# Streaming encoder step on 8 cores: the sums of squares of an RMS norm are joined on GpSimd ahead of one averaging matmul, and the planner's tables change with it

## The reference

```python
def rms_norm(x, g):
    y = x * rsqrt(mean(x * x, axis=-1, keepdims=True) + EPS)
    return y * g

def trunk_layer(x, c, ...):
    sh_m, sc_m, gt_m, sh_f, sc_f, gt_f = split(dot(silu(c), w_ada) + b_ada, 6)
    h = rms_norm(x, g_mix) * (1 + sc_m) + sh_m
    z = dot(h, w_in)                      # p | u | v
    u, v = gelu(z_u), layer_norm(gelu(z_v))
    mix = dot(concat([pool_mixer(p), u * (w_s v + b_s)]), w_out)
    x = x + gt_m * mix
    h = rms_norm(x, g_ffn) * (1 + sc_f) + sh_f
    x = x + gt_f * dot(silu(dot(h, w_gate)) * dot(h, w_up), w_down)
# after four layers: y = rms_norm(x, g_final)
```

## Time and profile before

| what | value |
|---|---|
| median of 3 runs | 2673.65 us (2672.88 to 2675.32) |
| the profiled execution | 2672.88 us |
| its span on core 0, the slowest | 2671.3 us |
| spans of the even cores | 2671.3, 2670.2, 2668.7, 2667.3 us |
| spans of the odd cores | 2661.4, 2661.7, 2662.1, 2660.4 us |
| busy on core 0 | PE 97%, DVE 62%, ACT 39%, POOL 8% |

### The profile page before, as it was taken

The page is one execution under the profiler, slowest core; times in us unless marked ns, Lnnn a source line. Parts: engine busy times, 40 slices in busy tenths (PEclk is TensorE's granted clock), DMA queues, the critical chain, the costliest instruction groups (busy, mean ns, idle before and its releaser), DMA issues.

```text
span 2671.3 us, 51741 instructions; the slowest of 8 cores (2660.4 to 2671.3 us)
## 1 busy us (share of the span) xinstructions
PE 2600.9 (97%) x18083; PEld 1575.1 (59%) x18083; DVE 1658.1 (62%) x3481; ACT 1032.0 (39%) x1737; POOL 216.6 (8%) x382
## 2 busy tenths in 40 slices
PE   5899999999999999999999999999999999999997
PEld 4666655555577655555557655555556765545645
DVE  2898654445789854444679885444467986444457
ACT  3676211113678611111477741111167872111144
POOL 2111000000001100000001110000001110000022
PEclk9999999999999999999999999999999999999999
DMA  9943653451010364551201055456101023111112
GB/s 182 210 80 62 116 98 64 80 95 33 1 37 5 89 124 80 93 97 18 48 1 37 5 116 112 80 96 111 32 1 36 6 53 64 29 32 28 29 48 84
DMA packets 31398, 174.23 MB, mean 65 GB/s; under 512 B 3696, under 2 KB 5424, under 8 KB 16544
## 3 DMA queue, kind: packets, MB, share of 16 engines
q0 software_dynamic: 23744, 148.87, 30.1%
q1 hardware_dynamic: 6704, 20.37, 2.4%
q10 hardware_dynamic: 688, 1.61, 0.2%
HBM read 302.41 MB, written 9.67 MB: 117 GB/s over the span
## 4 chain that ended last, share of the span: by engine, by line
PE 91%; DMA 2%; issue 2%; DVE 2%; ACT 1%; POOL 1%; POOLq 0%; DVEq 0%; ACTq 0%
PE bank L655 91%; DMA rows<-b_s 2%; ACT heap L878 0%; DMA wps<-w_ps 0%; DVE heap L870 0%; DVE x_sb L903 0%; DVE heap L835 0%; DVE x_sb L914 0%; POOL heap L647 0%; ACT heap L830 0%; DVE heap L875 0%; POOL rv L1003 0%; DVE heap L1102 0%; POOL rv L1005 0%; DVE heap L909 0%
## 5 line engine op out<-in xcount | busy, mean ns | idle before, releaser
L655 PE MATMUL bank<-heap 128*128 128x512 bf16 (+5 forms) x15272 | 2502.3, 326 | 9.6 <-DVE heap L1102 2.6
L655 PEld LDWEIGHTS bank<-heap 128*128 128x128 bf16 (+1 forms) x15272 | 1456.6, 98 | 998.3 <-issue 23.6
L903 DVE SCALAR_TENSOR_TENSOR x_sb<-bank,modT,x_sb 128x256 f32<-128x256 f32 (+2 forms) x1216 | 705.2, 592 | 497.7 <-PE bank L655 495.0
L1206 ACT ACTIVATE heap<-bank 128x512 bf16<-128x512 f32 (+4 forms) x447 | 228.9, 516 | 1253.6 <-PE bank L655 1139.9
L1208 DVE TENSOR_TENSOR heap<-heap,bank 128x512 bf16<-128x512 bf16 (+4 forms) x447 | 262.2, 587 | 287.4 <-PE bank L655 266.6
L878 ACT ACTIVATE heap<-heap,modT,gsc 128x256 bf16<-128x256 f32 (+1 forms) x335 | 174.0, 579 | 61.7 <-DVE heap L870 45.1
L870 DVE TENSOR_TENSOR heap<-x_sb,heap 128x512 f32<-128x512 f32 (+1 forms) x272 | 168.5, 655 | 38.4 <-ACT heap L854 24.4
L835 DVE TENSOR_TENSOR heap<-heap 128x512 f32<-128x512 f32 (+3 forms) x300 | 156.9, 542 | 30.2 <-ACT heap L830 21.7
L830 ACT ACTIVATE heap<-x_sb 128x1024 f32<-128x1024 f32 (+3 forms) x119 | 120.7, 1025 | 98.9 <-DVE x_sb L903 60.6
L1003 POOL TENSOR_SCALAR rv<-mv 128x1 f32<-128x1 f32 (+1 forms) x68 | 24.5, 360 | 740.0 <-DVE mv L1002 692.2
L661 ACT ACTIVATE heap<-bank 128x512 bf16<-128x512 f32 (+3 forms) x126 | 70.5, 588 | 34.0 <-PE bank L655 28.6
(11 more groups left out here) (80 smaller groups left out, 897.9 us busy)
## 6 DMA issues: line engine op xcount, KB each, us to landing
heap<-w_ada POOLq DMA_DIRECT2D x47, 1024.0 KB, 9.3
heap<-w_gate POOLq DMA_DIRECT2D x15, 1024.0 KB, 8.8
heap<-w_up POOLq DMA_DIRECT2D x15, 1024.0 KB, 13.0
heap<-w_down POOLq DMA_DIRECT2D x15, 1024.0 KB, 17.3
heap<-w_in POOLq DMA_DIRECT2D x9, 1024.0 KB, 11.1
heap<-w_out POOLq DMA_DIRECT2D x8, 1024.0 KB, 10.4
heap<-crow SPq DMA_DIRECT2D x15, 512.0 KB, 6.0
y_out<-heap SPq DMA_DIRECT2D x14, 512.0 KB, 2.6
```

Of the source, the lines that this page charges most:

```text
L655: r = e.matmul(s[0], s[1], s[2], start=s[3], stop=s[4], **(s[5] if len(s) > 5 else {}))
L903: dve(lambda e: e.scalar_tensor_tensor(out=xv, in0=B(bk)[:, 0:np_], scalar=modT[:, m, base + n, 0:1], in1=xv, op0=ALU.mult, op1=ALU.add), ...
L1206: act(lambda e: e.activation(out=sv(), in_=B(bks[0])[:, 0:N], func=AF.Silu), 0.067 + N / 1200, [bks[0].res[0]], [sg.res[0]], "silu")
```

## The change

Two tables of numbers change, and no code. The one number that changes what is computed where is ADD, from 4 to 8 in both roles:

```diff
     0: dict(RES_MIX=44000, RES_FFN=20000, RATE_A=0.7, RATE_B=0.6, HOLD=2, BOOST=20.0, SCARCE=1, SWITCH=6.0,
-            SLACK=2.0, LEAD_S=16.0, LEAD_H=10.0, LEAD_F=4.0, ADD=4, BUS0=12.5, FILL=2.2, HM0=4,
+            SLACK=1.0, LEAD_S=16.0, LEAD_H=4.0, LEAD_F=2.0, ADD=8, BUS0=12.5, FILL=2.2, HM0=4,
```

More of the change, by code:

```diff
@@ L22 @@
 CONST = {
-    0: dict(RES_MIX=44000, RES_FFN=20000, RATE_A=0.7, RATE_B=0.6, HOLD=2, BOOST=20.0, SCARCE=1, SWITCH=6.0,
-            SLACK=2.0, LEAD_S=16.0, LEAD_H=10.0, LEAD_F=4.0, ADD=4, BUS0=12.5, FILL=2.2, HM0=4,
+    0: dict(RES_MIX=40000, RES_FFN=20000, RATE_A=0.45, RATE_B=0.4, HOLD=2, BOOST=30.0, SCARCE=2, SWITCH=8.0,
+            SLACK=1.0, LEAD_S=16.0, LEAD_H=4.0, LEAD_F=2.0, ADD=8, BUS0=12.5, FILL=2.2, HM0=4,
             ORD0=(0, 1, 2, 3, 'x1', 'u', 'p', 'v', 'h', 'x2', 's', 'x3', 'o', 4, 5, 'x4', 'x5', 6, 7, 8, 9),
-            LEAD_Y=0.0, NSQ=2, LATE=100.0, MODV=(), MODP=7, PCSN=(3, 3, 4, 4, 4, 4), LASTP=(3, 4, 4, 4, 7),
+            LEAD_Y=0.0, NSQ=3, LATE=100.0, MODV=(), MODP=7, PCSN=(3, 3, 4, 4, 4, 4), LASTP=(3, 4, 4, 4, 7),
             NM=256, UNITS=(2, 2, 2, 2, 2, 2, 2, 1, 1)),
-    1: dict(RES_MIX=44000, RES_FFN=20000, RATE_A=0.55, RATE_B=0.3, HOLD=2, BOOST=30.0, SCARCE=3, SWITCH=5.0,
-            SLACK=2.0, LEAD_S=8.0, LEAD_H=4.0, LEAD_F=15.0, ADD=4, BUS0=12.5, FILL=2.2, HM0=4,
+    1: dict(RES_MIX=44000, RES_FFN=20000, RATE_A=0.6, RATE_B=0.4, HOLD=2, BOOST=30.0, SCARCE=4, SWITCH=6.0,
+            SLACK=1.0, LEAD_S=8.0, LEAD_H=7.0, LEAD_F=2.0, ADD=8, BUS0=12.5, FILL=2.2, HM0=4,
             ORD0=(0, 1, 2, 3, 'u', 'x1', 'p', 'h', 'v', 'x2', 's', 'o', 4, 5, 'x3', 'x4', 'x5', 6, 7, 8, 9),
-            LEAD_Y=0.0, NSQ=3, LATE=100.0, MODV=(3, 4, 5, 6, 7, 8, 9, 10, 11), MODP=7, PCSN=(3, 3, 4, 4, 4, 4),
+            LEAD_Y=0.0, NSQ=2, LATE=100.0, MODV=(3, 4, 5, 6, 7, 8, 9, 10, 11), MODP=8, PCSN=(3, 3, 4, 4, 4, 4),
             LASTP=(3, 4, 4, 4, 7), NM=272),
```

## The result

| | before | after |
|---|---|---|
| device time, median | 2673.35 us (2672.88 to 2675.32) | 2684.59 us over three executions, lowest 2684.03 |
| ratio after / before, 95% interval | | 1.0042 [1.0022, 1.0061] |
| span of core 0 in the profiled execution | 2671.3 us | 2666.0 us |
| span of core 1 | 2661.4 us | 2678.7 us |
| span of the slowest core | 2671.3 us (core 0) | 2684.2 us (core 5) |

What follows compares the result with a forecast made beforehand. PE on the even cores was taken to bound the kernel, 99.6% busy in the middle. Core 0's terms, -7.4 - 3.2 + 2.0 + 2.4 + 0.8 = -5.4 us, gave 2668.2 us against the median of 2673.65, range 2661 to 2679.

Steps and rivals of the forecast that it cites:

- averaging matmuls: Core 0: 79 averaging matmuls removed from PE, some six of them at waits saving nothing: -7.4 us.
- start, up to 160 us: Core 0: later first matmul mostly swallowed, then joins in the open at 76.44 and around 140: +2.0 us.
- wait for `rows`: Core 0, first handover: PE's matmuls between the two readers outlast the 7.5 us needed, so 3.2 us of idle time go.
- later handovers: Core 0, three handovers in the long middle: one join of 0.8 us in the open at each, +2.4 us.
- tail: Core 0, end: two joins ahead of POOL's four L1412 make them start and end later, +0.8 us.
- Rival 1: Joins on POOL lock DVE for up to 57 us, a fifth reaching PE: slower, 2679 us; chance 0.15.
- Rival 2: Joined chains gate PE so often that removed matmuls save nothing: +2.0, 2675.7 us, about 2671 with lower bounds; chance 0.15.
- The prediction's last test: Sign that the forecast is wrong: an odd core as the slowest; no size given.

Runs made afterwards that it cites:

- c_after: The changed kernel again, nothing altered, on another chip: odd cores 2682.3 us, even 2669.6, ratio to the kernel before 1.0017 [0.9965, 1.0070].
- e1: Changed kernel with the odd cores' table of before (two averaging matmuls, no join): odd cores 2666.9 us, even 2671.4, ratio to before 0.9997.
- f3: Changed kernel with odd cores' joins only in layers 1 and 2, two averaging matmuls elsewhere, replanned: odd cores 2662.9 us, even 2670.4, ratio to before 0.9995.
- f4: Changed kernel with odd cores' joins only ahead of feed-forward parts, two averaging matmuls in mixers and final norm: odd cores 2673.4 us, even 2668.9.
- e8: Changed kernel with two averaging matmuls and no join (ADD=4) on the odd cores alone: odd cores 2664.2 us, even 2672.4, ratio to before 0.9972.
- e4: Changed kernel with three buffers of squares instead of two (NSQ=3) on the odd cores: odd cores 2672.8 us, even 2675.6, ratio to before 1.0005.
- e2: Kernel before, tables of both roles kept except ADD=8 (join and one averaging matmul): odd cores 2680.7 us, even 2687.1, ratio to before 1.0049.
- e3: Changed kernel, new tables in both roles but ADD=4 (no join, two averaging matmuls): odd cores 2658.3 us, even 2683.4.
- f1: Changed kernel, same order, join replaced by a copy of the first half's sum: odd cores 2674.2 us, even 2662.1, ratio to before 1.0011.
- f2: Changed kernel, same order, join done as four additions of a quarter each: odd cores 2704.9 us, even 2699.6, ratio to before 1.0120.
- e5: Changed kernel with the join on VectorE in place of GpSimd, replanned: odd cores 2671.8 us, even 2681.0.
- e6: Changed kernel with only the planner's price of the join raised to 1.04 us for 256 columns, replanned: odd cores 2676.1 us, even 2700.0.

## Why the prediction was wrong

**The sum for the even cores held, at least as a sum.** Its steps against core 0's rows, in us:

| step | forecast | measured |
|---|---|---|
| averaging matmuls | -7.4 | PE busy -6.3, with 29 idle matmuls more |
| start, up to 160 us | +2.0 | idle +3.1 |
| wait for `rows` | -3.2 | idle from 160 to 300: -2.2 |
| later handovers | +2.4 | idle in the middle: +1.1 |
| tail | +0.8 | idle -1.0 |
| sum | -5.4 | -5.3 |

The same places on core 0 of the changed kernel, as answers to the earlier trace rows:

```profile
26.89 0.37 PE L655 MATMUL bank<-heap,meanb 128*128 128x256 bf16 x1 [26.89 <-POOL heap L846]
...
79.02 0.27 PE L655 MATMUL bank<-heap,meanb 128*128 128x256 bf16 x1 [2.19 <-POOL heap L846]
...
145.47 0.37 PE L655 MATMUL bank<-heap,meanb 128*128 128x256 bf16 x1 [2.38 <-POOL heap L846]
...
265.42 0.39 PE L655 MATMUL bank<-rows,oner 1*128 1x512 bf16 x1
```

PE's first matmul was put at 26.2 and came at 26.89: the first join took 0.84 us, near the 0.8 of the forecast, but began at 25.79 and not at 25.3. The wait for `rows` is gone, as the count of matmuls between its two readers said. In the later runs with the changed even cores they gained 1 to 2 us and not 5 (c_after, e1, f3, f4), or lost 1 (e8) or 3 (e4), so the exact agreement is partly luck. So is the sign, as e2 and e3 show: the joins cost this role 15 us under the old table, and the new table without them costs 11; the forecast had no term for how well the planner's order fits. The sum had 0.8 us a join and let it count in five or six places. By f1 and f2 it counts for 38 us per us of join on these cores.

**The step that failed** is the sentence on the odd cores: "On core 1 the same matmuls give -8, but its first handover now has only 14 matmuls of 512, 3.2 us, against a need of 7.5: a new wait of 4.3. It stays near 2660, below the even cores." It had two terms, which add up to 2657.7 and not to near 2660. The start, the handovers and the tail, which the sum for core 0 did price, were put at nothing without a reason, and the new wait for `rows` that it did name is only 1 us longer than the old one (2.6 where it was 1.6). In place of the missing terms the runs showed that the joins cost the odd cores 17 to 24 us under either table (e2, e3, e8). On core 1, against the same table without joins, 6 us lie in the mixer of the first layer, 5 in that of the last and 8 in the tail; the fewer matmuls win 5 back in between. PE's busy time shows none of the 8 us that were to be saved. Near 2660 was also only 8 us below the forecast for the even cores, less than the joins' cost. How the loss at each place divides between the length of the join and the order that the planner found with it stays open. Reading rows of core 1 at 135 to 165 us and in the last 60 us would have shown that its mixers have the least to put beside a chain: its PE waited 1.89 us for L835 at 146.72, and now 3.93 for L846 at 150.42.

**The tail of an odd core** is its own case. On core 1 of the changed kernel both engines come to work on L1412 at once:

```profile
2654.31 5.09 POOL L1412 TENSOR_TENSOR heap<-heap 128x1024 f32<-128x1024 f32 x2 [1.03 <-ACT heap L854]
...
2654.47 5.48 DVE L1412 TENSOR_TENSOR heap<-heap 128x512 f32<-128x512 f32 x2 [1.46 <-ACT heap L854]
...
2661.34 4.91 PE L655 MATMUL bank<-heap 128*128 128x128 bf16 x56 [4.88 <-DVE heap L1208]
```

These two of VectorE take 5.48 us where four took 0.69 each before. An L1208 stands behind them in VectorE's list, and 56 matmuls wait 4.88 us for it. Here the Trainium skill's rule ("SBUF — State Buffer", Who interferes with whom) does what the prediction cited it for, at L1412. At the joins VectorE loses much less, the 6.8 us in 22 operations of core 1 told above. The meeting at L1412 comes from the order and not from the length of the join: f1 has it too (2.74 and 2.82 us, and a wait of 4.69 for L1208), and so has e5 with its joins on VectorE (2.73 and 2.82, and 6.24). e8, e4, e6, f3 and f4 don't have it; there no L1412 of VectorE takes more than 0.70 us. It isn't all of the tail's loss, since e4 still loses 6 us there.

**The rivals.** Rival 1, at 2679, came nearest to the time and had joins beside VectorE right, but for the most part the wrong victim. It held 57 us of VectorE's time for possible; measured are 6.8 us on core 1 and 13.1 on core 0, and the medians of L870 and L1109 on core 5 are 0.683 and 0.681 us where they were 0.684 and 0.682 on core 1 before. More often the joins sit out VectorE's operations, 20 us over their 0.73 us on an odd core, and PE waits for the joins. Rival 2's case, removed matmuls paid back at the waits, is nearly what core 1 shows: no busy time saved, and 3.5 us more at the first wait and 3.4 at the others where it waits for the squares' sum. But it waits for a join in 15 places and not in every unit. Rival 2's lower figure was wrong in itself: with the lower bounds of the last three terms the sum is -7.2, which is 2666.5 and not about 2671. The prediction's last test, "or an odd core as the slowest", is the one that came in.

## What to carry to other kernels

In a program with several roles, work out the whole sum for each role whose distance to the slowest is smaller than the largest term; a role that is 0.4% ahead is not safe from a change that lengthens each of its chains. Price a step in a chain by its mean beside the engine that it shares with, and try what a longer and a shorter step cost in the same order of work before you trust a count of the places where it lies open: here two fifths to a half of it did. Then look at where the time went: a test that explains the size of a loss need not have touched the places where it arose. And where a planner lays the program out, a table is good only together with the operation it was found for: swapping one number in it, or the price of one operation, moved a role by 9 to 30 us.

## What was not expected of the hardware

- An addition on GpSimd of 128x256 float32 took 0.73 us alone and up to 3.38 us beside VectorE. By the times it waited for four of VectorE's operations in succession and not for one, and ended 0.58 us after the last. A GpSimd copy with one input, 0.40 us alone, did the same (3.06 us, ending 0.25 us after the last).
- In the wait of 3.93 us for a join PE's granted clock fell to 0.50, the lower of its two levels (1.2 GHz), and it came back some 7 us later on core 1 and some 14 us later on core 5. A late join can so cost its own wait and then double the time of the matmuls behind it. It isn't peculiar to joins: e8, without them, has 0.50 from 145 to 150 us. Core 1 of the changed kernel:

```profile
150.00:155.00 5.00, 3.33 (x52) 3.04 (x53) 4.55 (x10) 3.26 (x6) 0.28 (x1) 0.50 1.01 169
```
